# An attention stage whose four groups run one merged order per engine, taken from a list schedule

## The reference

```
q, k, v, xbc, z, dt_raw = jnp.split(h @ w_in, ...)
q = apply_rope(q) * HEAD_DIM ** -0.5 ;  k = apply_rope(k)
attn = mixture_of_dilations(q, k, v)      # causal, three dilation patterns
y    = ssd_chunked_scan(silu(conv(xbc)), ...) * silu(z) ...
out  = concat([attn, y]) @ w_out
```

## Time and profile before

| | us |
|---|---|
| median of three runs | 2705.45 (2705.3 to 2708.07) |
| profiled execution | 2703.95 |
| its span | 2701.8 |
| attention stage, from the end of the first group's v projection to the next stage | 878.5 to 1369 |

### The profile page before, as it was taken

One profiled execution on the slowest core, in us unless ns is written; L12 is line 12 of the kernel. 1 busy time (PEld: TensorE's weight loads), 2 busy tenths in 40 slices (PEclk: granted clock), 3 DMA queues, 4 the chain that ended last, 5 costly groups with the idle time before them and its releaser, 6 DMA issues. The chain is left out here.

```text
span 2701.8 us, 29157 instructions
## 1 busy us (share of the span) xinstructions
PE 2424.9 (90%) x10790; PEld 1949.8 (72%) x10790; DVE 1481.2 (55%) x2015; ACT 719.9 (27%) x989; POOL 301.1 (11%) x216
## 2 busy tenths in 40 slices
PE   6999999999968787787899967899599999999994
PEld 5888888888846565566777845687378888888883
DVE  5544444444483666666567266887844444444436
ACT  4111111111141445444422243312321111111112
POOL 3000000000031222222200033600300000000001
PEclk8999999999978999999999978999799999999997
DMA  4111111111031000000011221311411111111103
GB/s 158 46 51 47 47 47 47 47 47 47 31 126 40 16 24 17 24 16 32 16 55 52 97 101 71 125 47 48 170 47 47 47 47 47 49 60 47 47 8 124
DMA packets 34837, 152.35 MB, mean 56 GB/s; under 512 B 4048, under 2 KB 4688, under 8 KB 27984
## 3 DMA queue, kind: packets, MB, share of 16 engines
q1 hardware_dynamic: 34768, 151.48, 15.6%
HBM read 130.43 MB, written 21.04 MB: 56 GB/s over the span
## 5 line engine op out<-in xcount | busy, mean ns | idle before, releaser
L325 PE MATMUL psum<-norm_hi,gate_up_hi 128*128 128x512 f32 x1408 | 555.0, 394 | 46.6 <-DVE norm_lo L259 41.6
L326 PE MATMUL psum<-norm_lo,gate_up_hi 128*128 128x512 f32 x1408 | 553.0, 393 | 0.0
L327 PE MATMUL psum<-norm_hi,gate_up_lo 128*128 128x512 f32 x1408 | 552.6, 392 | 0.0
L395 DVE TENSOR_TENSOR acc<-psum,acc 128x512 f32<-128x512 f32 x432 | 291.0, 688 | 142.3 <-PE psum L370 140.8
L325 PEld LDWEIGHTS psum<-norm_hi,gate_up_hi 128*128 128x128 f32 x1408 | 267.4, 190 | 111.2 <-issue 34.5
L368 PE MATMUL psum<-act_hi,tile_hi 128*128 128x512 f32 x832 | 326.2, 392 | 13.3 <-DVE acc L392 8.4
L369 PE MATMUL psum<-act_lo,tile_hi 128*128 128x512 f32 x832 | 325.4, 391 | 0.0
L370 PE MATMUL psum<-act_hi,tile_lo 128*128 128x512 f32 x832 | 325.3, 391 | 0.0
L327 PEld LDWEIGHTS psum<-norm_hi,gate_up_lo 128*128 128x128 f32 x1408 | 267.4, 190 | 56.4
L326 PEld LDWEIGHTS psum<-norm_lo,gate_up_hi 128*128 128x128 f32 x1408 | 267.7, 190 | 55.4
L455 DVE TENSOR_TENSOR gate_scaled<-psum,rstd_rows 128x512 f32<-128x512 f32 x88 | 60.8, 691 | 449.4 <-PE psum L327 439.3
(11 more groups left out here) (226 smaller groups left out, 3771.6 us busy)
## 6 DMA issues: line engine op xcount, KB each, us to landing
raw_gate_up<-in_gu SPq DMA_DIRECT2D x44, 1024.0 KB, 4.9
raw_tile<-in_d SPq DMA_DIRECT2D x44, 512.0 KB, 3.5
raw_tile<-in_w_xz SPq DMA_DIRECT2D x19, 512.0 KB, 3.4
x_scratch<-acc SPq DMA_DIRECT2D x16, 512.0 KB, 2.9
cum_rows<-cum_scratch SPq DMA_DIRECT2D x8, 1024.0 KB, 4.6
raw_tile<-in_w_out SPq DMA_DIRECT2D x16, 512.0 KB, 3.5
x_stream<-x_scratch SPq DMA_DIRECT2D x16, 512.0 KB, 4.1
raw_tile<-in_w_att SPq DMA_DIRECT2D x11, 512.0 KB, 3.3
```

The source lines that it names most:

```text
L325: pe.matmul(o, guh[:, slot, m, k, :], nh[:, k, x], start=(k == 0), stop=False)
L326: pe.matmul(o, guh[:, slot, m, k, :], nl[:, k, x], start=False, stop=False)
L327: return pe.matmul(o, gul[:, slot, m, k, :], nh[:, k, x], start=False, stop=(k == KT - 1))
L395: v.tensor_tensor(a_, b_, a_, ALU.add).then_inc(sem(p + "_acc"), 1)
```

## The change

`att_events` and its weights go. `attention_plan` lists all steps of all four groups at once, each with an engine, a cost in microseconds, and the steps that it needs (data, free banks, free buffers). The steps of one kind form a line that keeps its order. Then a greedy loop picks, over all engines, the line's head that can start earliest; on a tie a rank decides (PE: score, then turn, then values, the fill last). What each engine got, in that order, is `ORDER`, and each engine's code is written out from it over the whole stage. There is no loop over groups left, and a step of the next group may stand ahead of the last steps of this one. On DVE and POOL the extra increments `at_softmax_go` and `at_norm_go` go, and DVE's wait for `at_norm` ahead of the masked minimum. The weight slots alternate over all tiles (`w % 2`, before `t % 2` within a group), and the tiles of the next stage are part of the same line of fill.

```
+            for f in range(len(last)):
+                w = f + 3
+                if f:
+                    weights(w, last[f - 2] if f > 1 else None)
+                for h in range(NH2):
+                    for q in range(PARTS):
+                        add("PE", "fill", ("part", f, h, q), 0.68, ("w_lo", w) if f and q + h == 0 else None,
+                            bank if q == 0 else None)
...
+                add("PE", "score", ("score", g, i, hh), 0.114 * w if w > 1 else 0.18,
+                    ("max", *SCORES[n - 2]) if n > 1 else None, ("qk_lo", g, hh + 1) if g and i == 0 else None,
+                    ("turn", *UNITS[u - 2], UNITS[u - 2][1]) if u > 1 else None)
+                add("DVE", "max", ("max", g, i, hh), 0.14 + 0.125 * w, ("score", g, i, hh))
+                add("ACT", "exp", ("exp", g, i, hh), 0.27 + 0.105 * w, ("max", g, i, hh))
+                add("DVE", "recip", ("recip", g, i, hh), 0.17, ("exp", g, i, hh))
+                add("POOL", "norm", ("norm", g, i, hh), 0.34 + 0.086 * w, ("recip", g, i, hh))
...
+                add("PE", "turn", ("turn", g, i, j), 0.62, ("norm", g, i, 3), ("low", *BLOCKS[n - 2]) if n > 1 else None)
+                add("ACT", "high", ("high", g, i, j), 0.58, ("turn", g, i, j),
+                    ("values", *BLOCKS[n - 2]) if n > 1 else None)
+                add("DVE", "low", ("low", g, i, j), 0.69, ("high", g, i, j))
+                add("PE", "values", ("values", g, i, j), 0.46, ("low", g, i, j), ("v_lo", g),
+                    ("end", *UNITS[u - 1]) if u else None)
...
+            rank = {("PE", "score"): 1, ("PE", "turn"): 2, ("PE", "values"): 3, ("PE", "fill"): 9, ("DVE", "pieces"): 1,
+                    ("DVE", "weights"): 8, ("ACT", "weights"): 8}
+            at_, free, end, order = dict.fromkeys(lines, 0), {}, {}, {}
+            while True:
+                best = None
+                for (engine, line), todo in lines.items():
...
+                    ready = max([end[x] + 0.15 for x in after], default=0)
+                    key = (round(max(free.get(engine, 0), ready), 3), rank.get((engine, line), 5), ready)
+                    if best is None or key < best[0]:
+                        best = key, engine, line, step
...
+                free[engine] = key[0] + (0.1 if engine == "SP" else cost)
+                end[step] = key[0] + cost + (0.2 if engine == "PE" else 0)
+                order.setdefault(engine, []).append(step)
...
-            last = due = None
-            for e in att_events(more):
-                if due and e[0] not in ("part", "xpart", "piece", "w", "xw"):
-                    values(*due)
-                    due = None
...
+            for step, *e in ORDER["PE"]:
+                if step == "score":
+                    score(*e)
+                elif step == "turn":
+                    turn(*e)
+                elif step == "values":
+                    values(*e)
...
             def soft(g, i, hh):
...
-                wait(v, "at_norm", n - 3)
-                v.sem_inc(sem("at_softmax_go"), 1)
-                v.wait_ge(sem("mask_in"), 16)
...
-            att_pe(pe, 0, True, True)
-            with pe.Fori(1, KVH - 1) as g:
-                att_pe(pe, g, False, True)
-            att_pe(pe, KVH - 1, False, False)
+            att_pe(pe)
```

More of the change, by code:

```diff
@@ L544, in cnt @@
             return sum(x + 1 for x in range(i)) + j
[L546 to L594, removed]
@@ L687, in v_pe, with att_pe, score @@
             mm.then_inc(sem("v_mm"), 1)
-        def att_pe(pe, g, first, more):
-            def score(i, hh):
+        def att_pe(pe):
+            def score(g, i, hh):
                 n = 32 * g + 4 * i + hh
@@ L704, in score, with turn @@
                 mm.then_inc(sem("at_score"), 1)
[L706 removed]
+            def turn(g, i, j):
                 n = NT * g + cnt(i, j)
@@ L765, in first_group_act @@
         def first_group_act(act):
-            att_w_hi(act, 0, 2)
+            att_w_hi(act, 2)
             act.wait_ge(sem("v_in"), 16)
             act.copy(vwh[:], vraw[:]).then_inc(sem("v_w_hi"), 1)
-            att_w_hi(act, 0, 3)
+            att_w_hi(act, 3)
             act.wait_ge(sem("turn_out"), past("t2", "out"))
[L771 to L789, removed]
@@ L791, in att_act, with own, qk_hi @@
-        def att_act(act, g, first, more):
-            def soft(i, hh):
+            for n in range(5):
+                qk_hi(act, 0, n)
+        def own(hh):
+            return slice(64 * (hh % 2), 64 * (hh % 2) + 64)
+        def qk_hi(act, g, n):
+            if n == 0:
+                act.wait_ge(sem("at_sum"), 6 * g + 6)
+                wait(act, "at_score", 32 * g)
+                act.copy(kh[:], qn[:, 2, :]).then_inc(sem("at_qk_hi"), 1)
+            else:
+                act.copy(qst[own(n - 1), n - 1, :], qn[own(n - 1), (n - 1) // 2, :]).then_inc(sem("at_qk_hi"), 1)
@@ L797, in soft @@
                    .then_inc(sem("at_exp"), 1)
[L799 to L803, removed]
-                        act.wait_ge(sem("v_read"), 2 * CH)
[L805 to L819, removed]
-                elif e[0] == "end":
-                    unit_end_act(act, g, e[1])
@@ L822, in att_act, with high @@
-            unit_end_act(act, g, CH - 1)
+            def high(g, i, j):
+                n = NT * g + cnt(i, j)
+                act.wait_ge(sem("at_t_mm"), n + 1)
+                wait(act, "at_pv", n - 1)
+                act.copy(pth[:, n % 2].rearrange("p a d -> p (a d)"), banks(4 + n % 2)).then_inc(sem("at_t_hi"), 1)
+            for step, *e in ORDER["ACT"]:
+                if step == "exp":
+                    soft(*e)
+                elif step == "high":
+                    high(*e)
+                elif step == "end_lo":
+                    unit_end_act(act, *e)
+                elif step == "qk_hi":
+                    qk_hi(act, *e)
+                elif step == "v_hi":
+                    if e[0] == 0:
+                        act.wait_ge(sem("v_read"), 2 * CH)
+                    wait(act, "at_pv", NT * e[0])
+                    act.copy(vg[:, :, 0, :], vall[:, :, e[0] * HD:(e[0] + 1) * HD]).then_inc(sem("at_v_hi"), 1)
+                elif e[0] <= LAST_AT_W:
+                    att_w_hi(act, e[0])
+                else:
+                    t = e[0] - LAST_AT_W
+                    if t < 2:
+                        act.wait_ge(sem("pj_mm"), 12 * KVH - 2)
+                    w_hi(act, "xz", t, t % 2, 2 * t - 2)
```

270 lines of the change are left out of this document (162 added, 108 removed).

## The result

The changed kernel takes 2619.28 us (median of four runs, 2618.86 to 2622.3) where the kernel before takes 2705.38 beside it: a ratio of 0.9682 (0.9669 to 0.9695), 86 us less. The forecast was 2644, with 2606 to 2682 as its range: sign and range hold, the gain is 25 us larger than the sum of 61.

What follows compares the result with a forecast made beforehand. PE was taken to bound the kernel, with 90 us idle in attention. 42 + 10 + 20 - 5 - 3 - 3 = 61 us, subtracted from the median of 2705.45, gave 2644 us; range 2606 to 2682.

Steps and rivals of the forecast that it cites:

- The bound, and what attention's end is worth: Whole span: PE, busy 90%, carries the kernel; every microsecond by which attention ends earlier ends the kernel earlier.
- Fill moved to the starts: First 40 us of each group: moved fill and overlapping blocks, 49 us of work, meet 48.5 us idle; 42 us won.
- The overlap of groups: Ends of groups 1 and 2: last blocks move behind the next group's first score, 13 us of PE work.
- The clock: Group starts: with the holes gone the granted clock stays up; 10 of at most 12 us won.
- The long units: Attention after each group's first 40 us: half of 41.2 us PE idle time goes, 20 us won; bounds 0 and 41.
- all idle time goes: Rival for attention: PE is busy throughout, 97 us won, 2608 us; chance 0.12.
- The stage's start: Start of attention: PE's first score waits for the first head's split; about 5 us lost, between 3 and 8.
- The stage's end: Last PE steps of attention: no fill there, one block's chain is exposed; 3 us lost, between 1 and 6.
- POOL and DVE side by side: Attention: DVE's two-input steps meet POOL's divisions; 14 us lost on these engines, 3 on the time; bounds 0 and 56.
- the slower rival: Ends of groups 1 and 2 and weight splits: POOL and DVE exclude each other; likely 2725 us, chance 0.05.
- Removed instructions and the loop: Increments, DVE's wait for `at_norm`, and the loop's entry and turn in attention: 0 won, at most 3 us.
- what was to show it: Attention signs: end near 1308, holes gone and clock 1.00 in groups 1 to 3, `values` waiting under 20 us for `low`.

Runs made afterwards that it cites:

- b_fence_even: Changed kernel, but a group's first score waits for the previous group's last `values`, and each fill part is released where the old even spread had it: 2625.68 us, ratio 0.9716.
- c_fence: Changed kernel, but a group's first score waits for the previous group's last `values`; the fill stays free: 2618.75 us, ratio 0.9692.
- e_start: Changed kernel, but in the plan the very first score waits for the first eight parts of fill: 2614.32 us, ratio 0.967.

## Why the prediction was right, and where its steps failed

*The bound, and what attention's end is worth*: right. PE carries the span, the stage behind shows the same 176 of 182 us, and nothing took the place of what was won.

*Fill moved to the starts, 42 us*: the size of the idle time was right, its cause was wrong. This is the step that failed. Putting the fill back and parting the groups costs 9 us (0.9716 against 0.9682), not 42. (The 9 hold beside the new order of the chains; beside the old one it was not run.) The step was wrong where it put the idle time of 40 us windows down to short units with too little fill beside them. The one after 1004 holds 13 us of the true start and then 27 us of units 0 to 3, at a clock of 1.00, where, by the reading above, the old lists asked for `low` and for minima too early. A cut at the work's own borders would have parted the two: 7.0 us idle in the start, which the change got down to 1.6, and 8.45 in units 0 to 3, which `b_fence_even` got down to 1.43 with no more fill there.

*The overlap of groups*, 13 us of work within that step: about 0 (`c_fence`).

*The clock, 10 us*: PE's busy time fell by 21. The clock rose from 0.96 to 0.98 in the stage, 2% of 400, about 8 us. The rest is seen in the means of instructions whose work is the same: `values` 470 ns before and 444 now, scores 384 and 356. They are drawn longer where they follow a wait (a `values` 0.50 us behind a wait of 0.76 at 1074.43, against 0.40 at 1111.12); how much of that is real time on the engine these rows don't say. Idle time and busy time fell for one reason, and the sum counted only the first and the clock.

*The long units, 20 us, half of 41*: mis-sized. `b_fence_even` won 13.2 us in units 4 to 7 of one group (65.3 to 52.1), of which 7.3 are idle time and the rest fewer and shorter records; idle in units 4 to 6 fell from 8.69 to 1.44. The idle time there went nearly whole, as in the rival "all idle time goes". The 1.88 us for a round through one of two banks was no obstacle to that; what was wrong was the weight given to the lower bound, by which a different order on DVE "meets as many". `values` waits 0.9 for `low`, `turn` 9.0.

*The stage's start, -5*: `e_start` gets back 5.0 by the medians, 3 by the ratios. The wait stood at 878.09 with 3.10 us, as written. Right within what can be told.

*The stage's end, -3*: 1.00 + 0.56 + 0.55 + 0.17 = 2.3 us of waits from 1278 on. Right.

*POOL and DVE side by side, 14 us on those engines, 3 on the time*: the first is seen. DVE's weight splits went from 1224 to 1624 ns in the mean (14 of them, 5.6 us), its splits of q from 1220 to 1321 (1.6), POOL's divisions by 4.9 - 1.6 = 3.3 us: 10.5 in all against 14. (Before, the odd heads' took 51.2 us and the even heads' 45.4.) Lines after, of DVE and then of POOL:

```profile
L531 DVE TENSOR_TENSOR tile_lo<-raw_tile,tile_hi 128x1024 fp32r<-128x1024 f32 x14 | 22.7, 1624 | 1.9 <-ACT tile_hi L806 0.9 <-ACT tile_hi L527 0.8
L834 DVE TENSOR_TENSOR q_hi_lo<-q_k_next,q_hi_lo 64x1024 fp32r<-64x1024 f32 x16 | 21.1, 1321 | 0.5
L997 POOL TENSOR_SCALAR probs_odd<-probs_odd,denom_recip 128x256 f32<-128x256 f32 (+3 forms) x64 | 56.1, 883 | 102.4 <-DVE denom_recip L940 102.3
L997 POOL TENSOR_SCALAR probs_even<-probs_even,denom_recip 128x128 f32<-128x128 f32 (+3 forms) x64 | 43.8, 694 | 108.0 <-DVE denom_recip L940 107.9
```

What it costs the time was not tried by itself. PE's waits for POOL itself are 0.2 us; but at the end of group 2, the place that the slower rival named, the split of q took 6.60 us and not 4.97 beside two divisions of 1024 columns, which took 4.15 together:

```profile
1165.02 4.15 POOL L997 TENSOR_SCALAR probs_odd<-probs_odd,denom_recip 128x1024 f32<-128x1024 f32 x2 [4.84 <-DVE denom_recip L940]
...
1166.14 6.60 DVE L834 TENSOR_TENSOR q_hi_lo<-q_k_next,q_hi_lo 64x1024 fp32r<-64x1024 f32 x4
```

PE's longest wait, told below, ends behind that split, so up to 1.6 us of it are the exclusion's. The rival had a right mechanism at the right place, once, and at a fraction of its price; and PE waited there for its bank, not for the division as the rival had it. The Trainium skill, "SBUF — State Buffer", "SBUF: two separate sides", has such a pair exclude each other for the whole instruction; the longer means agree, and the 50 us that full exclusion of every step would have cost did not come.

*Removed instructions and the loop, 0, at most 3*: 6 us, of which 3.5 (1 to 6) are the loop's. Mis-sized, some 3 us beyond its bound. The Trainium skill, "Runtime: NRT & Kernel Launch", "Instruction fetch mechanics", has a taken branch stall the fetch when its target lies outside the pages held; 3.5 us for one loop of two turns on four engines agree with a small price of that kind, though no row parts it from the registers and branches themselves.

Of what was to show it: attention ended at 1285, earlier than 1308; the holes of 4 to 5 us are gone (all waits of scores for a minimum together are 2.7 us); the clock was 1.00 over the 40 us from the first scores of groups 1 to 3 on (986.0, 1075.9, 1182.4), though not just ahead of the last of them; divisions of 512 columns are longer (692 ns before, 814 now), those of 384 shorter (652 and 585), those of 128 and 256 the same. One hole is new, and I had not foreseen it: a part of the next stage's fill waits 4.17 us for its bank, which DVE empties only behind the split of q that lasts from 1166.14 to 1172.74, the longest wait left, 9 us ahead of group 3's first score (1182.44), with the clock at 0.56 behind it. So the split of q still opens a hole at the start of group 3, at another place. The clock is 0.69 over 11 us here (1172 to 1183) and at the stage's start (874.9 to 886), and 0.99 to 1.00 in the rest of the stage. Timeline, and the windows around it:

```profile
1173.58 0.80 PE L688 MATMUL psum<-norm_hi,tile_hi 128*128 128x512 f32 x1 [4.17 <-DVE staged_conv_in L953]
```
```profile
1170.00:1175.00 5.00, 1.42 (x3) 1.17 (x4) 4.63 (x7) 0.10 (x1) 1.12 (x1) 0.75 0.00 0
1175.00:1180.00 5.00, 5.00 (x18) 4.19 (x17) 0.22 (x1) 0.77 (x2) 0.00 (x0) 0.56 0.00 0
1180.00:1185.00 5.00, 5.00 (x31) 4.35 (x30) 2.55 (x12) 2.18 (x7) 0.37 (x1) 1.00 0.00 0
```

Put together: +6 for code, +80 for the lists, of which some 70 for the order of the chains' steps, which needs PE's and DVE's lists both, and some 8 for the fill's place; the start and the end cost the 5 and 2 that were named and are in these sums. The prediction had them as 42 for fill and overlap and 20 for the chains. It came within 25 us since both draw on the same 90 us of idle time; with the larger term put down to the wrong cause, that the range holds is in part luck.

## What to carry to other kernels

Where several engines walk one shared list of events, count for each chain how much of the consumer's own work the list puts between a step and the one that needs it, and compare it with the chain's time in the timeline, queues of the engines between included. If it is less, give each engine its own order, and change the engines of the chain together: here one engine's new list gave a quarter of the gain (DVE's, 21 of 80), and new lists on all but DVE a loss of 5, hardly clear of noise. What the distance itself does is the part that was only read from the lists. And cut windows at the borders of the work, since a window of fixed length puts idle time down to whatever it is named after.

## What was not expected of the hardware

The clock fell behind waits much shorter than the holes of the earlier trace rows. Windows of `b_fence_even` at the start of group 1:

```profile
987.00:990.00 3.00, 2.98 (x16) 2.39 (x14) 1.78 (x3) 0.81 (x1) 0.00 (x0) 1.00 0.00 0
990.00:993.00 3.00, 0.94 (x6) 0.85 (x6) 2.65 (x11) 1.13 (x5) 0.86 (x1) 0.98 0.00 0
993.00:996.00 3.00, 3.00 (x13) 2.39 (x12) 2.40 (x16) 2.55 (x11) 2.28 (x6) 0.50 0.00 0
996.00:1000.00 4.00, 4.00 (x25) 3.70 (x24) 3.19 (x14) 3.42 (x10) 2.38 (x5) 0.97 0.02 4
```

PE had been busy for 2.98 of 3 us at 2.4 GHz; two waits of 0.91 and 1.17 us left it 0.94 us of work in three, and the next three went at 1.2 GHz, with PE busy in all of them. So this start has a clock of 0.78 with 4.8 us idle, and the kernel before 0.84 with 7.0: in this kernel short waits in place of one hole did not save the clock. And a loop of two turns, whose price no wait in the profile showed, cost 3.5 us (1 to 6) when it was all that differed.
